# Expert rows are scaled at eviction and added into one table of token rows by an accumulating indirect DMA

## The chip, the cores and the metric

One core of one Trainium2 chip runs the whole program. The metric is the device time of one execution in microseconds; the median of three executions of the kernel before is 1866.39 us (1865.68 to 1872.32).

## What is computed

One step of a one-layer encoder for 1024 prompt tokens and 64 sample tokens (T = 1088 rows of 1024 float32). Three attention branches are mixed into a residual `h`; then comes a mixture of experts and a last normalisation. What matters here is the mixture: every token goes to 2 of 32 experts, each expert is a SwiGLU of width 512, and the two results are added to `h` with weights.

```python
def channel_mixer(h, g, w_coarse, b_coarse, w_fine, b_fine, wg, wu, wd):
    ht = rmsnorm(h, g).reshape(B * T, D)
    idx, wts = hier_route(ht, w_coarse, b_coarse, w_fine, b_fine)   # 2 experts and 2 weights for each token
    return h + moe_experts(ht, idx, wts, wg, wu, wd).reshape(B, T, D)
...
def expert_block(args):
    xblk, e = args
    return (jax.nn.silu(xblk @ wg[e]) * (xblk @ wu[e])) @ wd[e]
...
y_prompt = rmsnorm(hp, norm_final)
y_sample = rmsnorm(hs, norm_final)
```

## The kernel before, in words

The program is written in stages, each ended by a barrier of all engines. The change touches the last two.

**Mixing and routing, then the experts** (one stage, from L1736). Tokens come in nine tiles (`NT`), eight of 128 rows and one of 64. For each tile TensorE makes `h` (`project`, two halves), VectorE adds the residual into `mixT` (or `hlast` for the ninth tile), and the two engines with ScalarE normalise it (`nrow`), write it to a DRAM table `ffn_rows` and route it: `choose` finds the two experts and the logits' differences `lgd` and `dif`, `count` and `take` find the place of the token in each expert's list (`rk`, and `which`, a one-hot row over 128 places), and `enlist` multiplies `which` with `tokoh`, the token's number at its expert's column, and sums over all tiles in one PSUM bank, `TB`. At the end `toks` holds for each expert (column) the token number of each of its 128 places. A place that no token took holds 0, and so names token 0. The exponentials of `lgd` and `dif` and from them the weights `wts` are made once for all tiles, the latter in `overflow`, during the expert loop.

**Expert loop.** 32 experts, each one page of 128 places. GpSimd (POOL) gathers an expert's 128 rows from `ffn_rows` into `xe` by an indirect DMA (L1873), two buffers; TensorE turns them (`turn_x`), multiplies by gate and up weights (`up`), turns the hidden rows (`turn_h`) and multiplies by the down weights (`down`) of the expert before. Every product is made of three float32r products, so each weight is split into a high part (`hig`, ScalarE, `split_high`) and a low part (`low`, VectorE, `split_low`). SyncE's queue (SP) loads weights in halves of 1 MB into a ring of eight buffers `raw`, each load issued when TensorE has used the half eight before (`used`). ScalarE's `out` empties the banks of `down` into `ye` (two buffers), and its own queue stores the page to a DRAM table `expert_rows` (L2290). The last expert's page goes out in two halves (`last_out`). An expert with over 128 tokens would have further pages (`further`), of which there are up to 16; they are cleared with zeros by 16 DMAs early in the stage. In this case's inputs no expert has more than 128 tokens. The order within one pass is in the code of TensorE:

```python
for n in range(1, NE):
    up(n, "g", PA)
    turn_h(n - 1)
    up(n, "u", PB)
    if n + 1 < NE:
        turn_x(n + 1)
        down(n - 1)
```

**Last stage** (from L2653). POOL gathers for each token tile two tables of rows from `expert_rows`, one for each chosen expert (`ya`, `yb`, L2679, places in `sidx`); VectorE multiplies and adds them to `h` (`add`, two instructions), ScalarE makes the mean square, logarithm and exponential, VectorE scales (`scale`), SP stores.

Of the kernel before, what the change touches and what calls it, by code (L numbers as in the profile page):

```python
# [22 lines left out]
P = 128  # L23
# [4 lines left out]
NT = 9  # L28
# [48 lines left out]
def build(nc, io, stop_after=99):  # L77
# [6 lines left out]
    ysd = nc.dram_tensor("expert_rows", (SLOTS, D), F32).ap()  # L84
# [1594 lines left out]
    zfill = at("zfill", [P, SLOTS // P + 2], I32, f + 2272)  # L1679
# [11 lines left out]
    which = [at("which", [P, 2, P], F32, OS + 49152 + 1024 * i) for i in range(2)]  # L1691
    tokoh = [at("tokoh", [P, 2, NE], F32, OS + 51200 + 256 * i) for i in range(2)]
# [29 lines left out]
    toks = at("toks", [P, NE], I32, f + 32)  # L1722
    tcur = at("tcur", [P, 1], I32, f + 288)
    ye = [at("ye", [P, D], F32, o5 + 4096 * i) for i in range(2)]
# [11 lines left out]
    with Stage(nc) as ctx:  # L1736
# [5 lines left out]
            logged, picked, ranked, taken, placed, listed, filled, consts, kept0, kept1, expd, counted, found, again, halved, offset, gained, lastcopied = sems(  # L1742
                ctx, "rt", "router_in gain_in wo_high wo_low x0 x1 thigh tlow mixed hdone sq_done rooted ndone hturned ncopied "
                "logged picked ranked taken placed listed filled consts kept0 kept1 expd counted found again halved offset "
                "gained lastcopied")
        named, f0, f1, xturned, xhigh, xlow, used, high, lowed, silued, multiplied, gturned, hhigh, hlow, emptied, s0, s1, lefthalf, halfout, \
            *loaded = sems(ctx, "x", "named f0 f1 xturned xhigh xlow used high lowed silued multiplied gturned hhigh hlow "
                           "emptied s0 s1 lefthalf halfout " + " ".join(f"l{i}" for i in range(RAW)))
# [4 lines left out]
        fetched, stored = [f0, f1], [s0, s1]  # L1753
# [6 lines left out]
        def further(eng, body):  # L1760
# [3 lines left out]
            with eng.If(many > 0):  # L1764
                if eng.engine == nc.gpsimd.engine:
# [5 lines left out]
                    eng.wait_ge(again, 16 * 2 * NT)  # L1771
# [9 lines left out]
        def _(sp):  # L1781
            for i in range(STEPS):
# [26 lines left out]
            for t in range(2, NT):  # L1809
                sp.wait_ge(sq_done, t - 1)  # L1810
                sp.dma_start(xt[t % 2][0:rows_of(t), :], xp[t * P:t * P + P, :] if t < FULL else xs[:, :]).then_inc(x_in[t % 2], 16)
            sp.wait_ge(mixed, 2 * NT)
            for q in range(3, len(halves)):
                if q >= RAW:
                    sp.wait_ge(used, q - RAW + 1)
# [12 lines left out]
        def _(pool):  # L1828
# [11 lines left out]
            with pool.Fori(0, OVER) as b:  # L1840
                dst = ysd[bass.ds(b * P + NE * P, P), :].rearrange("p (a c) -> p a c", c=256)
                pool.dma_start(dst, nil[:, :].unsqueeze(1).to_broadcast([P, D // 256, 256])).then_inc(cleared, 16)
            pool.wait_ge(cleared, 16 * OVER)
# [901 lines left out]
```

## Time and profile before

| | |
|---|---|
| median of three executions | 1866.39 us |
| span of the profiled execution | 1870.5 us |
| expert loop, first to last page emptied | about 1249 to 1820 us |
| last stage | 1824 to 1870.5 us |
| TensorE busy | 1779.2 us (95%) |
| VectorE busy | 1045.1 us (56%) |
| ScalarE busy | 869.0 us (46%) |
| GpSimd busy | 115.1 us (6%) |
| bytes moved by DMA | 329.85 MB |

The profiled execution lies within the range of the three timed ones (its span of 1870.5 us is 4.1 us above their median). TensorE's busy share counts overlapping matmuls, so where it is full only means that no gap is seen. A DMA share is the time that packets took, divided by 16 engines and the stretch; it can read slightly above 1.

### The profile page before, as it was taken

To read this page: it belongs to the slowest core of one execution; us is meant where nothing else is said; L and a number is where in the kernel's file an instruction comes from. 1 tells how busy PE (TensorE), PEld (TensorE's weight loads), DVE (VectorE), ACT (ScalarE), POOL (GpSimd) and SP (SyncE) were. 2 spreads that over 40 slices of the span, in tenths; PEclk is the share of its full clock that TensorE was granted. 3 is DMA by queue.
4 is the path that set the end of the run, shared out by engine and by line. 5 is a ranking of instruction groups with operands and counts; after the bars stand their busy time and mean duration, and the time that the engine had idled before them with its cause. 6 is when DMAs were issued, how large, how long until landed. Compare 5 with 4: busy or idle time off the path is not lost. (4 is left out here: it accounts for less than half of the span.)

```text
span 1870.5 us, 25656 instructions
## 1 busy us (share of the span) xinstructions
PE 1779.2 (95%) x10354; PEld 1569.0 (84%) x10354; DVE 1045.1 (56%) x1275; ACT 869.0 (46%) x1122; POOL 115.1 (6%) x138
## 2 busy tenths in 40 slices
PE   9998999999999999999999999989999999999990
PEld 7886777888898879999999998878888888888870
DVE  5325665343245432132332245658898998988967
ACT  4224555323263331121122222247788788787853
POOL 0020000000000021000000000010000101000003
PEclk9998999999999999999999999989999999999995
DMA  5241110112112226111112142159999999999968
GB/s 186 85 110 29 29 30 12 48 34 61 34 36 81 68 59 210 40 52 45 40 48 83 46 172 71 63 212 392 414 420 410 414 410 421 418 410 416 416 232 297
DMA packets 139322, 329.85 MB, mean 176 GB/s; under 512 B 13675, under 2 KB 91335, under 8 KB 114502
## 3 DMA queue, kind: packets, MB, share of 16 engines
q1 hardware_dynamic: 123556, 272.69, 39.3%
q0 software_dynamic: 10896, 38.74, 5.6%
q10 hardware_dynamic: 4752, 16.78, 2.2%
q8 instruction: 84, 1.38, 0.3%
q14 instruction: 34, 0.27, 0.0%
HBM read 286.08 MB, written 39.87 MB: 174 GB/s over the span
## 5 line engine op out<-in xcount | busy, mean ns | idle before, releaser
L2479 DVE TENSOR_TENSOR low<-raw,hig 128x2048 fp32r<-128x2048 f32 x192 | 431.7, 2287 | 57.6 <-ACT hig L2214 57.2
L2214 ACT ACTIVATE hig<-raw 128x2048 fp32r<-128x2048 f32 x192 | 359.2, 1915 | 24.0 <-ACT ye L2287 14.4
L2042 PE MATMUL bank<-hig,xel 128*128 128x512 f32 x512 | 202.8, 396 | 0.0
L2044 PE MATMUL bank<-hig,xeh 128*128 128x512 f32 x512 | 199.9, 390 | 0.0
L2043 PE MATMUL bank<-low,xeh 128*128 128x512 f32 x512 | 199.5, 390 | 0.0
L71 PE MATMUL bank<-xhi,glo 128*128 128x384 f32 (+1 forms) x552 | 180.8, 328 | 3.2 <-ACT sg L2148 1.8
L73 PE MATMUL bank<-xhi,ghi 128*128 128x384 f32 (+1 forms) x552 | 180.8, 327 | 0.0
L72 PE MATMUL bank<-xlo,ghi 128*128 128x384 f32 (+1 forms) x552 | 180.5, 327 | 0.0
L71 PE MATMUL gproj<-xhi,glo 128*128 128x384 f32 (+1 forms) x384 | 132.6, 345 | 0.0
L72 PE MATMUL gproj<-xlo,ghi 128*128 128x384 f32 (+1 forms) x384 | 127.6, 332 | 0.0
L73 PE MATMUL gproj<-xhi,ghi 128*128 128x384 f32 (+1 forms) x384 | 127.5, 332 | 0.0
L2044 PEld LDWEIGHTS bank<-hig,xeh 128*128 128x128 f32 x512 | 96.2, 188 | 20.6
L2042 PEld LDWEIGHTS bank<-hig,xel 128*128 128x128 f32 x512 | 96.7, 189 | 19.0
L2043 PEld LDWEIGHTS bank<-low,xeh 128*128 128x128 f32 x512 | 96.4, 188 | 19.0
L2377 DVE TENSOR_TENSOR tm<-sg,bank 128x384 f32<-128x384 f32 (+1 forms) x42 | 22.3, 531 | 153.7 <-PE bank L73 153.7
L71 PEld LDWEIGHTS bank<-xhi,glo 128*128 128x128 f32 x552 | 104.2, 189 | 3.6 <-DVE glo L2351 2.0
L72 PEld LDWEIGHTS bank<-xlo,ghi 128*128 128x128 f32 x552 | 104.2, 189 | 0.0
L73 PEld LDWEIGHTS bank<-xhi,ghi 128*128 128x128 f32 x552 | 104.1, 188 | 0.0
L2068 PE MATMUL bank<-hig,htl 128*128 128x512 f32 x256 | 102.4, 400 | 0.0
L2070 PE MATMUL bank<-hig,hth 128*128 128x512 f32 x256 | 100.0, 391 | 0.0
L2069 PE MATMUL bank<-low,hth 128*128 128x512 f32 x256 | 99.9, 390 | 0.0
L2148 ACT ACTIVATE sg<-bank 128x384 f32<-128x384 f32 (+1 forms) x63 | 29.5, 471 | 142.9 <-PE bank L73 135.7
(425 smaller groups left out, 3594.5 us busy)
## 6 DMA issues: line engine op xcount, KB each, us to landing
raw<-in_w_e_gate_dram SPq DMA_DIRECT2D x64, 1024.0 KB, 7.8
raw<-in_w_e_up_dram SPq DMA_DIRECT2D x64, 1024.0 KB, 8.2
raw<-in_w_e_down_dram SPq DMA_DIRECT2D x64, 1024.0 KB, 7.4
graw<-in_w_in_dram SPq DMA_DIRECT2D x39, 512.0 KB, 3.8
expert_rows<-ye ACTq DMA_DIRECT2D x31, 512.0 KB, 8.1
xt<-in_x_prompt_dram SPq DMA_DIRECT2D x16, 512.0 KB, 3.6
expert_rows<-nil POOLq DMA_DIRECT2D x16, 512.0 KB, 10.3
braw<-in_w_branch_dram SPq DMA_DIRECT2D x24, 256.0 KB, 2.8
```

The costliest lines, as they stand in the source:

```text
L71: nc.tensor.matmul(out, wl, xh, start=(i == 0), stop=False)
L72: nc.tensor.matmul(out, wh, xl, start=False, stop=False)
L73: last = nc.tensor.matmul(out, wh, xh, start=False, stop=(i == len(parts) - 1))
L2042: nc.tensor.matmul(bank[:, :], xel[n % 2][:, kk, :], wh[:, k, :], start=(kk == 0), stop=False)
L2043: nc.tensor.matmul(bank[:, :], xeh[n % 2][:, kk, :], wl[:, k, :], start=False, stop=False)
L2044: last = nc.tensor.matmul(bank[:, :], xeh[n % 2][:, kk, :], wh[:, k, :], start=False, stop=(kk == KC - 1))
L2068: nc.tensor.matmul(bank[:, :], htl[n % 2][:, kk, :], wh[:, k, cols], start=(kk == 0), stop=False)
L2069: nc.tensor.matmul(bank[:, :], hth[n % 2][:, kk, :], wl[:, k, cols], start=False, stop=False)
L2070: last = nc.tensor.matmul(bank[:, :], hth[n % 2][:, kk, :], wh[:, k, cols], start=False, stop=(kk == 3))
L2148: nc.scalar.activation(gate_of(i, g)[:, 0:m], src[:, 0:m], ACT.Sigmoid).then_inc(gated, 1)
L2214: nc.scalar.activation(hig[q % HI][:, :], raw[q % RAW][:, :], ACT.Copy).then_inc(high, 1)
L2479: nc.vector.tensor_tensor(low[q % RAW][:, :], raw[q % RAW][:, :], hig[q % HI][:, :].bitcast(F32), ALU.subtract).then_inc(lowed, 1)
```

## The change

1. **A table of token rows.** A DRAM tensor `token_rows` (`acc`, T + 128 rows) takes the place of `expert_rows`. SP stores `h` itself there, tile by tile (`h_store`, nine DMAs, eight of 512 KB and one of 256 KB). The last 128 rows are spare. The 16 clearing DMAs become one.
2. **Weights in the same list.** For each tile ScalarE makes the exponentials (`exponents`), VectorE the weights (`weights`, five small instructions), and `enlist` sums the weights beside the token numbers; the last tile's weights follow in `enlist_weights`. The result, `slotw`, has the weight of each place; an empty place has weight 0.
3. **Empty places are marked.** Token numbers are summed as number + 1, so 0 means empty; the empty place p gets row T + p, one of the spare rows. The gather has a bound (`bounds_check=T - 1`), so places with such a row aren't fetched. `xe` is cleared once before its first use.
4. **Eviction with weight, and addition by DMA.** `out` evicts with `scale=slotw[:, n:n + 1]`, and POOL adds the page into `token_rows` by an indirect DMA with `compute_op=ALU.add` (`add_rows`), all 128 places. Each addition waits for the one before it (`added`), the first for all of `h_store`; `out` waits for the addition from its `ye` buffer.
5. **Last stage.** SP loads nine plain tiles from `token_rows`; VectorE's two instructions for `add` go.

```diff
+            def h_store(n, sem):
+                sp.dma_start(wide(acc[n * P:n * P + rows_of(n), :]), hrow(n, rows_of(n))).then_inc(sem, 16)
...
+            def add_rows(n):
+                pool.wait_ge(emptied, n + 1)
+                if n:
+                    pool.wait_ge(added, 16 * n)
+                else:
+                    pool.wait_ge(hkept, 16 * NT)
+                pool.indirect_dma_start(acc, bass.IndirectOffsetOnAxis(ap=toks[:, n:n + 1], axis=0), ye[n % 2][:, :], None,
+                                        compute_op=ALU.add).then_inc(added, 16)
             pool.wait_ge(named, 1)
             for n in range(NE):
                 if n >= 2:
                     pool.wait_ge(xturned, 2 * n - 2)
+                if n == 1:
+                    pool.wait_ge(listed, NT + 1)
+                    nc.gpsimd.memset(xe[1][:, :], 0.0).then_inc(cleanx, 1)
+                    pool.wait_ge(cleanx, 1)
                 pool.indirect_dma_start(xe[n % 2][:, :], None, htd,
-                                        bass.IndirectOffsetOnAxis(ap=toks[:, n:n + 1], axis=0)).then_inc(fetched[n % 2], 16)
+                                        bass.IndirectOffsetOnAxis(ap=toks[:, n:n + 1], axis=0),
+                                        bounds_check=T - 1, oob_is_err=False).then_inc(fetched[n % 2], 16)
+                if n >= 4:
+                    add_rows(n - 4)
+            for n in range(NE - 4, NE):
+                add_rows(n)
...
             def out(n):
                 if n >= 2:
-                    act.wait_ge(stored[n % 2], 16 * (n // 2))
+                    act.wait_ge(added, 16 * (n - 1))
+                else:
+                    act.wait_ge(scaled, 1)
                 act.wait_ge(used, place["d", n, 1] + 1)
                 for half in range(2):
-                    last = nc.scalar.activation(ye[n % 2][:, half * 512:half * 512 + 512], [Z0, Z1][half][:, :], ACT.Copy)
+                    last = nc.scalar.activation(ye[n % 2][:, half * 512:half * 512 + 512], [Z0, Z1][half][:, :], ACT.Copy,
+                                                scale=slotw[:, n:n + 1])
                 last.then_inc(emptied, 1)
-                act.wait_ge(emptied, n + 1)
-                act.dma_start(ysd[n * P:(n + 1) * P, :], ye[n % 2][:, :]).then_inc(stored[n % 2], 16)
...
+            def weights(n):
+                R = slice(0, rows_of(n))
+                ve.wait_ge(expd, n + 1)
+                nc.vector.scalar_tensor_tensor(out=wts[R, n, 0:1], in0=dif[R, n:n + 1], scalar=1.0, in1=tot[R, n:n + 1],
+                                               op0=ALU.add, op1=ALU.mult)
+                ve.drain()
+                nc.vector.reciprocal(wts[R, n, 0:1], wts[R, n, 0:1])
+                ve.drain()
+                nc.vector.tensor_tensor(wts[R, n, 1:2], wts[R, n, 0:1], dif[R, n:n + 1], ALU.mult)
+                ve.drain()
+                for k in range(2):
+                    last = nc.vector.tensor_scalar(tokoh[n % 2][R, k, NE:2 * NE], oh[R, k, n, :], wts[R, n, k:k + 1], None, ALU.mult)
+                last.then_inc(portioned, 1)
...
+            for t in range(NT):
+                r = rows_of(t)
+                sp.dma_start(ya[t][0:r, :], acc[t * P:t * P + r, :]).then_inc(ys_[t], 16)
+                if t == 0:
+                    sp.dma_start(gf[:, :], io["norm_final"].partition_broadcast(P)).then_inc(g_in, 16)
...
-            for t in range(NT):
-                r = rows_of(t)
-                for k, dst in enumerate((ya, yb)):
-                    pool.indirect_dma_start(dst[t][0:r, :], None, ysd,
-                                            bass.IndirectOffsetOnAxis(ap=sidx[k][0:r, t:t + 1], axis=0)).then_inc(ys_[t], 16)
```

POOL's program at the start of the expert loop, before: after the last tile's `ffn_rows` it holds only gathers into the two `xe` buffers, to the end of the loop.

```order
L1865 DMA ffn_rows<-nrow_7317 64x1024
L1873 DMA xe_7389<-ffn_rows,toks_7399 128x1024
L1873 DMA xe_7390<-ffn_rows,toks_7399 128x1024
L1873 DMA xe_7389<-ffn_rows,toks_7399 128x1024
L1873 DMA xe_7390<-ffn_rows,toks_7399 128x1024
```

The same place of the changed kernel (`token_rows<-ye` is an addition):

```order
L1886 DMA ffn_rows<-nrow_7317 64x1024
L1907 DMA xe_7390<-ffn_rows,toks_7400 128x1024
L1905 MEMSET xe_7391 128x1024
L1907 DMA xe_7391<-ffn_rows,toks_7400 128x1024
L1907 DMA xe_7390<-ffn_rows,toks_7400 128x1024
L1907 DMA xe_7391<-ffn_rows,toks_7400 128x1024
L1907 DMA xe_7390<-ffn_rows,toks_7400 128x1024
L1897 DMA token_rows<-ye_7406,toks_7400 1216x1024
L1907 DMA xe_7391<-ffn_rows,toks_7400 128x1024
L1897 DMA token_rows<-ye_7407,toks_7400 1216x1024
```

Each addition of page n now stands on POOL between the gathers for experts n + 4 and n + 5, and a clearing instruction stands ahead of the second gather.

VectorE at the end of routing, before: `take` of the eighth tile, the residual's last half, and, eighteen rows of the last `choose` and `take` later, the list.

```order
L2417 TENSOR_TENSOR nrow_7317<-hlast_7320,gb_7316 64x512
L2465 TENSOR_TENSOR prod_7349<-bank,oh_7331 128x64
L2467 TENSOR_TENSOR ohs_7343<-ohs_7343,oht_7344 128x32
L2469 TENSOR_REDUCE rk_7332<-prod_7349 128x2
L2472 TENSOR_SCALAR which_7364<-iot_7345,rk_7332 128x128 x2
L2397 TENSOR_TENSOR hlast_7320<-xt_7314,bank 64x512
...
L2542 CAST toks_7399<-bank 128x32
L2479 TENSOR_TENSOR low_7377<-raw_7369,hig_7385 128x2048
```

The same places of the changed kernel:

```order
L2474 TENSOR_TENSOR nrow_7317<-hlast_7320,gb_7316 64x512
L2522 SCALAR_TENSOR_TENSOR wts_7324<-dif_7335,tot_7361 128x1
L2525 RECIPROCAL wts_7324<-wts_7324 128x1
L2527 TENSOR_TENSOR wts_7324<-wts_7324,dif_7335 128x1
L2530 TENSOR_SCALAR tokoh_7367<-oh_7331,wts_7324 128x32 x2
L2536 TENSOR_TENSOR prod_7349<-bank,oh_7331 128x64
...
L2618 TENSOR_SCALAR miss_7401<-bank,empty_7404 128x32
L2620 SCALAR_TENSOR_TENSOR toks_7400<-bank,miss_7401 128x32
L2522 SCALAR_TENSOR_TENSOR wts_7324<-dif_7335,tot_7361 64x1
L2525 RECIPROCAL wts_7324<-wts_7324 64x1
```

Five small instructions of `weights` now stand ahead of `take` and of the residual's last half, the list takes two instructions instead of one, and the last tile's `weights` follow it.

## Rows read from the trace of the kernel before

**Rows 1.** The page's part 2: DMA share in 40 slices of 46.8 us.
```profile
DMA  5241110112112226111112142159999999999968
```

**Rows 2.** Stretches: engines' busy us, then PE clock, DMA share, GB/s.
```profile
1236.00:1249.00 13.00, 8.40 (x44) 7.62 (x44) 7.37 (x19) 3.56 (x4) 3.53 (x3) 0.74 1.00 410
1843.00:1855.00 12.00, 0.00 (x0) 0.00 (x0) 11.70 (x11) 4.94 (x12) 3.74 (x5) 0.50 1.03 421
...
1430.00:1500.00 70.00, 70.00 (x331) 58.61 (x331) 63.98 (x50) 56.10 (x47) 6.29 (x4) 1.00 1.01 413
```

**Rows 3.** Timeline of SP's queue: start, us; two gate loads of successive experts.
```profile
1403.39 3.05 SPq L1816 DMA_DIRECT2D raw<-in_w_e_gate_dram  x2
...
1421.15 3.05 SPq L1816 DMA_DIRECT2D raw<-in_w_e_gate_dram  x2
```

**Rows 4.** DMA queues in 1290 to 1750: packets, MB, share of 16 engines.
```profile
q1 hardware_dynamic: 22398, 163.09, 86.3%
q0 software_dynamic: 3744, 13.63, 7.4%
q10 hardware_dynamic: 3690, 13.44, 7.2%
```

**Rows 5.** Timelines of ACT, DVE and PE: the gate weights of one expert.
```profile
1412.53 3.72 ACT L2214 ACTIVATE hig<-raw 128x2048 fp32r<-128x2048 f32 x2
...
1414.70 4.48 DVE L2479 TENSOR_TENSOR low<-raw,hig 128x2048 fp32r<-128x2048 f32 x2
...
1423.67 0.39 PE L2042 MATMUL bank<-hig,xel 128*128 128x512 f32 x1
```

**Rows 6.** DMA issues of the whole run: KB each, median us to landing.
```profile
expert_rows<-ye ACTq DMA_DIRECT2D x31, 512.0 KB, 8.1
xt<-in_x_prompt_dram SPq DMA_DIRECT2D x16, 512.0 KB, 3.6
...
xe<-ffn_rows,toks POOLq DMA_INDIRECT x32, 8.7
expert_rows<-ye ACTq DMA_DIRECT2D x2, 256.0 KB, 2.0
```

**Rows 7.** Timeline of POOL and PE, then landings of `xe` in 1240 to 1260.
```profile
1243.08 1.22 POOL L1873 DMA_INDIRECT xe<-ffn_rows,toks  x1 [6.61 <-DMA ffn_rows<-nrow]
...
1257.54 1.05 PE L2028 MATMUL bank<-ident,xe 128*128 128x128 f32 x8
...
DMA to landing us min/median/max: 4.5/5.7/5.9
```

**Rows 8.** Timeline of DVE at the end of routing, and the costliest POOL memset.
```profile
1230.24 0.22 DVE L2465 TENSOR_TENSOR prod<-bank,oh 128x64 f32<-128x64 f32 x1 [0.74 <-PE bank L1964]
...
1231.64 0.68 DVE L2397 TENSOR_TENSOR hlast<-xt,bank 64x512 f32<-64x512 f32 x1 [0.20 <-PE bank L1927]
...
1241.01 0.19 DVE L2542 CAST toks<-bank 128x32 int32<-128x32 f32 x1 [1.15 <-PE bank L1974]
...
L963 POOL MEMSET keep<- 128x1088 f32 x1 | 1.0, 1010 | 76.0 <-POOLq L65 76.0
```

**Rows 9.** Timelines of the end, in order of time, and POOL's load of `ovi`.
```profile
1814.43 1.09 ACT L2287 ACTIVATE ye<-bank 128x512 f32<-128x512 f32 x2 [2.21 <-PE bank L2070]
...
1820.43 0.34 ACTq L2302 DMA_DIRECT2D expert_rows<-ye  x1
...
1824.06 0.33 SPq L2667 DMA_DIRECT2D gf<-in_norm_final_dram  x1
...
1834.66 1.06 ACT L2688 ACTIVATE junk<-ya 128x1024 f32<-128x1024 f32 x1 [9.32 <-DVE ya L2702]
...
1836.25 0.20 ACT L2692 ACTIVATE stat<-stat 128x1 f32<-128x1 f32 x1
...
1865.27 1.28 DVE L2708 SCALAR_TENSOR_TENSOR yo<-ya,stat,gf 64x1024 f32<-64x1024 f32 x1 [0.65 <-ACT stat L2692]
...
L1763 POOLq TENSOR_LOAD <-ovi x1: 509/509/509, 1791.2 to 1791.2; - x1
```

More of the change, by code:

```diff
@@ L1860, in _ @@
             pool.sem_inc(consts, 1)
-            pool.dma_start(slot_tok.rearrange("(p a) one -> p (a one)", p=P), zfill[:, :]).then_inc(filled, 16)
+            pages = slice(NE * P, SLOTS)
+            with nc.allow_non_contiguous_dma(reason="an index for each place of the overflow pages, once"):
+                pool.dma_start(slot_tok[pages, :].rearrange("(a p) one -> p (a one)", p=P), spare[:, :]).then_inc(filled, 16)
+            pool.dma_start(slot_w[pages, :].rearrange("(p a) one -> p (a one)", p=P), nought[:, :]).then_inc(filled, 16)
             for t in range(NT):
@@ L1972, in enlist, with enlist_weights @@
                 pe.wait_ge(placed, n + 1)
+                cols = slice(0, 2 * NE if n < FULL else NE)
                 for k in range(2):
-                    last = nc.tensor.matmul(TB[:, 0:NE], which[n % 2][0:rows, k, :], tokoh[n % 2][0:rows, k, :],
-                                            start=(n == 0 and k == 0), stop=(n == FULL and k == 1), skip_group_check=True)
+                    last = nc.tensor.matmul(TB[:, cols], which[n % 2][0:rows, k, :], tokoh[n % 2][0:rows, k, cols],
+                                            start=(n == 0 and k == 0), stop=False, skip_group_check=True)
+                last.then_inc(listed, 1)
+            def enlist_weights():
+                pe.wait_ge(portioned, NT)
+                pe.wait_ge(named, 1)
+                for k in range(2):
+                    last = nc.tensor.matmul(TB[:, NE:2 * NE], which[FULL % 2][0:DEC, k, :], tokoh[FULL % 2][0:DEC, k, NE:2 * NE],
+                                            start=False, stop=(k == 1), skip_group_check=True)
                 last.then_inc(listed, 1)
@@ L2017, in _ @@
             keep(16)
+            enlist_weights()
             pe.wait_ge(kept[0], 16 * 5)
@@ L2248, in _ @@
                     norm(n - 1)
+                if 2 <= n < NT:
+                    exponents(n - 2)
                 if n + 1 < NT:
@@ L2254, in _ @@
                     half_square()
+                    exponents(FULL - 1)
                 if n == NT:
@@ L2524, in _ @@
                 if n >= 2:
+                    weights(n - 2)
                     take(n - 2)
@@ L2534, in _ @@
             last_gain(0)
+            weights(FULL - 1)
             take(FULL - 1)
```

146 lines of the change are left out of this document (76 added, 70 removed).

## The prediction

> **What bounds the kernel now.** I read the page's row of DMA shares first. It is low until the 26th slice and then at nine tenths or more to the end [rows 1]: the experts keep the DMA engines full. The table by stretches says how full. In 1430 to 1500 us TensorE is busy without a gap at full clock, and the DMA share reads 1.01 at 413 GB/s [rows 2]. Where nothing but DMA limits, the share reads 1.00 to 1.03 at 410 to 421 GB/s [rows 2]: 1236 to 1249, where five weight loads, a store and two gathers wait in the queues, and 1843 to 1855, where gathers and stores of the last stage run together. So both TensorE and DMA are at their limit in the loop, and the reader should see that DMA has at most 2% to spare. The timeline of SP's queue gives the period, 1421.15 - 1403.39 = 17.76 us for each expert [rows 3], and because TensorE shows no gap this period is TensorE's. The table of queues splits the DMA load of a period: weights (q1) 86.3%, gathers (q0) 7.4%, stores of `ye` (q10) 7.2%, together 100.9% [rows 4].
>
> How late may weights be? The gate halves of one expert are split from 1412.53 on; VectorE's pair starts at 1414.70 and its first half is done about 2.24 us later, at 1416.9. TensorE takes it at 1423.67 [rows 5]. So 6.7 us of lag are covered before TensorE stops.
>
> The end is a second, separate bound: from the issue of the last store, 1820.43, to the end of the span there are 50.1 us in which TensorE has nothing to do. In them the last stage starts at 1824.06 and VectorE's last scaling is done at 1866.55 [rows 9].
>
> **The change, part by part.** The sums are against the profiled span of 1870.5 us. It is 4.1 us (0.2%) above the median of 1866.4 us, and I carry the difference over to the median.
>
> *Expert loop, DMA.* The gather loses its empty places: two experts for each of 1088 tokens make 2176 rows, 68 of 128 places for each expert, so 7.4% becomes 3.9% if all DMA engines gain alike. The store of 512 KB becomes an addition, which no row shows. At least it costs what the store does, 7.2% [rows 4]. It must also read the row in DRAM that it adds to; if reads and the write are moved in turn by the engine, a read of the same size more makes it 14.4%. I take 14.4%, since weights (a read from DRAM and a write) and stores (the same in reverse) share the engines' time as if one stream of bytes went through [rows 2, 4]. Then a period asks 86.3 + 3.9 + 14.4 = 104.6%. Against the highest reading of a full queue, 103% [rows 2], the period is 17.76 x 104.6 / 103 = 18.04 us, 0.28 longer. Page 30 is emptied at 1815.5 [rows 9], so page 0 thirty periods earlier, at 1283; from there the additions load about 29 periods, 8.1 us in all, and 6.7 of these are covered: **+1.4 us**. Bounds: at 7.2% the sum is 97.4% and nothing is lost; at 14.4% against 101% the period is 18.39 us and the loss 18.3 - 6.7 = 11.6 us.
>
> The Trainium skill (Collectives: The Full Stack, Part 3, on why ReduceScatter is half of AllGather) says that the addition itself costs a DMA engine nothing but needs two source reads on the same ring, and gives a measured ratio of 1.93. By that, an estimate from the page, the addition would be 13.9% and the loss in the loop about nothing; no row of this trace shows an addition.
>
> *Expert loop, queues.* On POOL an addition stands between two gathers. The gather for expert n + 4 is issued when TensorE has turned the rows of n + 2, just ahead of `down(n)`; page n is emptied behind `down(n)`, and POOL waits there, queued in front of the gather for n + 5. The next gather is due a period after the last, so it waits only if the addition before, which must have landed, takes over 17.8 us. Gathers of the same size land in 8.7 us and stores in 8.1 in the full loop [rows 6]; with 1.3 us more (7.2% of 17.76) for the second read I expect 10. ScalarE's `out` needs the addition of two pages before: 35 us, covered. ScalarE loses a DMA issue (0.34 us) and is not the bound: **0 us**.
>
> *Routing.* `exponents` and `weights` stand beside projections that keep TensorE full, except at the end. There five small instructions come ahead of `take`. The five like them that `take` itself has lie in the 1.4 us from 1230.24 to the residual at 1231.64 [rows 8], so I price `weights` at 1.3 us; 0.74 us of it fills an idle time and 0.2 us another [rows 8], and the residual's half, with the chain to `nrow` and the last tile's routing behind it, is some 0.4 us later. The gather for expert 0 waits for the last tile's rows in DRAM, not for the list, which is there 1.9 us earlier (1241.20 against 1243.08 [rows 7, 8]); that covers the list's second instruction, 0.3 us. `h_store` adds 256 KB to the crowded queue, 0.6 us at 410 GB/s, against some 0.5 MB less of the first two gathers. **+0.7 us.** The clearing of `xe` (1.0 us by the memset of nearly its size [rows 8]) and the wait for `enlist_weights` move the second gather from just behind the first to about 1247; with the 5.7 us of a gather here it lands by 1253 and is first needed at 1257.5 [rows 7]. The 16 clearing DMAs that go lay under full TensorE work: 0 us.
>
> *The end.* Before, 50.1 us. After: page 30 is emptied at 1815.52 [rows 9]. An addition in an empty queue is not shown; a gather of this size outside the full loop takes 4.5 to 5.9 us from POOL's issue to landing, median 5.7 [rows 7]; with 1.3 us for the second read, 7.0. Additions go one after the other: 1822.5, then 1829.5 for page 31 (emptied at 1820.4, so it no longer goes out in halves). POOL then loads `ovi` (0.5 us [rows 9]) and branches, 0.9 us, which was done at 1791 before. From the last store's landing (1820.43 + 2.0 [rows 6, 9]) to SP's first issue at 1824.06 were 1.6 us: SP starts at 1832.0, 7.9 us later than before. A plain load of 512 KB lands in 3.6 us [rows 6], 1835.6. VectorE's additions are gone, so ScalarE is the slowest: 1834.66 to 1836.45 for one tile [rows 9], with the pause 1.84, times nine 16.6 us: 1852.2. Scaling 1.3 us, and 3.95 us from there to the end as before (1866.55 to 1870.5): 1857.4. **-13.1 us.** Bounds: additions of 4.5 us each give -18; of 12 us each, -3.1.
>
> Sum: 1.4 + 0 + 0.7 - 13.1 = **-11.0 us**, a span of 1859.5 and a median of **1855.4 us**.
>
> **The rivals.**
>
> *B, the gather's saving falls on the wrong engines.* A page fills from place 0. The reference's routing of these inputs gives 50 to 92 tokens for each expert, and the first 64 places are 96% full. If a fixed half of the DMA engines serves the first 64 places, these engines keep 7.1% of gather while they carry the whole addition: 86.3 + 7.1 + 14.4 = 107.8%, and a weight load is complete when its slowest engine is. Period 18.59, 29 x 0.83 - 6.7 = +17.3 us in the loop, total +4.9: **1871 us**. The same follows if the bound doesn't spare the empty places at all. For it speaks that DMA is full; against it, that no row shows which engine serves which place. The Trainium skill (DMA: Bandwidth & Descriptors, The descriptor swizzle) has this split, engines 0 to 7 for partitions 0 to 63, for a plain transfer of 1 MiB; the trace can't show it.
>
> *C, an addition costs well over two stores: slower.* With three, 86.3 + 3.9 + 21.6 = 111.8%, period 19.28, 29 x 1.52 - 6.7 = +37.4, and 2.6 more at the end: **1894 us**. The point from which the change loses: 11.7 us saved elsewhere and 0.7 spent, so a lag of 12.4 + 6.7 = 19.1 us, 0.66 a period, 106.8%, an addition of 16.6% or 2.3 stores. If landing takes over 17.8 us POOL's chain of additions becomes the period; at 20 us that is 29 x 2.2 = +65.
>
> *D, additions are slow to land but light on the engines.* At 12 us each in the empty queue the end saves 3.1 us only, the loop is as before: -2.4, **1864 us**.
>
> **How the numbers follow.** Half a per cent, 9.3 us, is about what a measurement of this kernel can tell from no change. My forecast has 0.45, with its own range of 1849 to 1861; B 0.20; C 0.20, to 1935; D 0.15. Faster than 1857.1: two thirds of the forecast's chance, 0.30. Slower than 1875.7: a third of B, nearly all of C, 0.27. Within: 0.43. The range leaves out the best tenth of the forecast and the upper half of C: 1850 to 1893 us.
>
> **What would show it.** The interval of SP's gate loads: 17.8 to 18.1 us with no gaps in TensorE beyond a few tenths is the forecast, 18.6 is B, over 19 C. The landings of `raw` should grow by up to 6.7 us if DMA lags. The share of q0, now gathers and additions: about 18%; 11% would mean that an addition costs one store. The landing of an addition: 10 us in the loop, 7 at the end; 12 at the end is D. The last stage: SP's first load at 1832 less the routing's and loop's shift, ScalarE's chain at 1.84 us a tile, 25 us from first load to end. TensorE's granted clock should stay full in the loop; if short stalls let it fall, the loss is larger than all the sums here, and that is where I'd be wrong first.

## The result, and the profile after

| | kernel before | changed kernel |
|---|---|---|
| median, us | 1869.4 (four runs, 1865.7 to 1873.2) | 1896.0 (four runs, 1890.0 to 1898.9) |
| ratio to before, 95% interval | | 1.0141 (1.0122 to 1.0161) |
| span of the profiled execution, us | 1870.5 | 1893.8 |
| issue of the first gather, us | 1243.08 | 1238.38 |
| the last page's `ye` is emptied, us | 1820.4 | 1848.65 |
| from there to the end, us | 50.1 | 45.15 |

The change makes the kernel 1.4% slower; 0.6% faster was forecast (11.0 us of 1866.4). The profile is read as the prediction reads that of before, and splits the 23.3 us by which the span grew. The expert loop begins 3.35 us earlier (TensorE first turns gathered rows at 1245.65 instead of 1249.00), its last page is emptied 28.25 us later, so the loop itself took 31.6 us more, and the end is 4.95 us shorter: -3.35 + 31.6 - 4.95 = +23.3.

**The loop.** The table by stretches, as in [rows 2]:

```profile
1290.00:1750.00 460.00, 440.39 (x2049) 362.51 (x2048) 392.55 (x270) 350.31 (x292) 97.00 (x49) 1.00 1.01 377
1430.00:1500.00 70.00, 66.56 (x313) 54.83 (x312) 60.58 (x48) 52.49 (x45) 13.96 (x8) 1.00 1.02 368
```

TensorE had no gap in 1430 to 1500 before; now it lacks 3.4 of 70 us. The DMA share is as high as where nothing but DMA limits [rows 2], and yet only 368 GB/s move, where 413 did. The clock granted is full. SP's gate loads, as in [rows 3]:

```profile
1329.10 3.05 SPq L1833 DMA_DIRECT2D raw<-in_w_e_gate_dram  x2
...
1346.85 3.05 SPq L1833 DMA_DIRECT2D raw<-in_w_e_gate_dram  x2
...
1364.61 3.05 SPq L1833 DMA_DIRECT2D raw<-in_w_e_gate_dram  x2
...
1383.52 3.05 SPq L1833 DMA_DIRECT2D raw<-in_w_e_gate_dram  x2
...
1402.27 3.05 SPq L1833 DMA_DIRECT2D raw<-in_w_e_gate_dram  x2
```

Up to 1364.61 the period is the old 17.75 us, then 18.9, 18.75, and so on; the 22 periods from 1383.52 to 1801.61, the 10th to the 32nd and last gate load, have 19.00 us on the mean (periods of other kernels below are taken over the same 22). Additions begin at 1280.2, so five periods went by before TensorE felt anything. That fits the covered lag of the prediction, used up at 19.0 - 17.75 = 1.25 us a period (6.7 / 1.25 = 5.4). What TensorE's suppliers waited for in 1430 to 1500 (us in total, times, longest) and the queues in 1290 to 1750, as in [rows 4]:

```profile
DVE low L2550 <- ACT hig L2280: 9.5, 13, 1.9
ACT hig L2280 <- DMA raw<-in_w_e_up_dram: 8.2, 7, 1.8
ACT hig L2280 <- DMA raw<-in_w_e_gate_dram: 7.3, 4, 2.3
...
ACT hig L2280 <- DMA raw<-in_w_e_down_dram: 2.2, 4, 0.9
```

```profile
q1 hardware_dynamic: 21103, 153.66, 83.5%
q0 software_dynamic: 6923, 19.31, 17.7%
...
raw<-in_w_e_down_dram SPq DMA_DIRECT2D x49, 1024.0 KB, 14.2
raw<-in_w_e_gate_dram SPq DMA_DIRECT2D x49, 1024.0 KB, 13.1
...
xe<-ffn_rows,toks POOLq DMA_INDIRECT x25, 8.9
token_rows<-ye,toks POOLq DMA_INDIRECT x24, 11.6
```

ScalarE waits for weights (TensorE has no wait for a gather in the list of 1290 to 1815). Gathers and additions (q0) take 17.7% of the engines' time; the forecast had 18%. An addition lands in 11.6 us, far below a period, so POOL's chain of additions is not what sets the pace. The trace also has a record for each packet that a DMA engine moved. Worked out from these records over the whole run (the packets of 4096 B fall into two groups, under and over 240 ns), median durations:

```
packets of 4096 B on q0, gather or plain store:  159 ns
packets of 4096 B on q0, addition:               327 ns
packets of 8192 B on q1, weights:                309 ns
```

A row's addition takes 327 / 159 = 2.06 times what a row's store takes. A place that the gather skips is not gone from the queue: it leaves a packet of 4 B that takes 9 ns (3264 packets of 4 B on q0 in the whole run, and 1360 in e1 below, whose gather skips nothing), so skipping does spare an engine nearly the whole row.

**The head and the end.** POOL's first two gathers and the first turn of rows, as in [rows 7], then the end in order of time, as in [rows 9]:

```profile
1238.38 4.14 POOL L1907 DMA_INDIRECT xe<-ffn_rows,toks  x1 [7.51 <-DMA ffn_rows<-nrow]
1242.52 0.97 POOL L1905 MEMSET xe<- 128x1024 f32 x1
1244.29 1.03 POOL L1907 DMA_INDIRECT xe<-ffn_rows,toks  x1 [0.80 <-POOL xe L1905]
...
1245.65 1.97 PE L2086 MATMUL bank<-ident,xe 128*128 128x128 f32 x8 [4.27 <-DMA xe<-ffn_rows,toks]
...
1844.31 1.55 POOL L1897 DMA_INDIRECT token_rows<-ye,toks  x1 [15.00 <-ACT ye L2355]
...
1851.03 1.54 POOL L1897 DMA_INDIRECT token_rows<-ye,toks  x1 [5.18 <-DMA token_rows<-ye,toks]
...
1866.18 0.33 SPq L2744 DMA_DIRECT2D ya<-token_rows  x1
...
1869.73 1.06 ACT L2759 ACTIVATE junk<-ya 128x1024 f32<-128x1024 f32 x1 [2.28 <-DMA ya<-token_rows]
...
1873.26 1.06 ACT L2759 ACTIVATE junk<-ya 128x1024 f32<-128x1024 f32 x1 [1.74 <-DMA ya<-token_rows]
...
1886.86 1.28 DVE L2772 SCALAR_TENSOR_TENSOR yo<-ya,stat,gf 64x1024 f32<-64x1024 f32 x1 [0.39 <-ACT stat L2763]
```

Between the landing of the last addition (about 1857, 6 us behind its issue as those before it) and SP's first load at 1866.18 stand some 9 us. The instructions of the line that ends the expert stage show with what:

```profile
L1742 POOLq DRAIN  x1: 6174/6174/6174, 1858.6 to 1858.6; - x1
```

POOL drains for 6.17 us. Before, the same drain took 3.56 us, but at 1792.5, 28 us ahead of the last page, where nothing waited for it.

### The profile page after: what moved, and what is told of

The parts are those of the page before. It is cut to its first block and busy times, and to the rows that moved or that the text cites. A ratio compares the mean times of both kernels' runs of the same rounds, so it can differ in the third digit from the quotient of the medians.

```text
span 1893.8 us, 25725 instructions
## 1 busy us (share of the span) xinstructions
PE 1784.5 (94%) x10358; PEld 1565.5 (83%) x10358; DVE 1037.7 (55%) x1301; ACT 877.0 (46%) x1147; POOL 167.0 (9%) x141
## 5 line engine op out<-in xcount | busy, mean ns | idle before, releaser
L2550 DVE TENSOR_TENSOR low<-raw,hig 128x2048 fp32r<-128x2048 f32 x192 | 437.5, 2288 | 83.2 <-ACT hig L2280 82.5
L2280 ACT ACTIVATE hig<-raw 128x2048 fp32r<-128x2048 f32 x192 | 367.3, 1918 | 124.4 <-DMA raw<-in_w_e_gate_dram 51.7
L2101 PEld LDWEIGHTS bank<-low,xeh 128*128 128x128 f32 x512 | 96.9, 189 | 18.5
L1897 POOL DMA_INDIRECT token_rows<-ye,toks x32 | 73.5, 2298 | 273.6 <-ACT ye L2355 268.5
```

Source lines behind the costliest of these rows:

```text
L1897: pool.indirect_dma_start(acc, bass.IndirectOffsetOnAxis(ap=toks[:, n:n + 1], axis=0), ye[n % 2][:, :], None, compute_op=ALU.add).then_inc ...
L2101: nc.tensor.matmul(bank[:, :], xeh[n % 2][:, kk, :], wl[:, k, :], start=False, stop=False)
L2280: nc.scalar.activation(hig[q % HI][:, :], raw[q % RAW][:, :], ACT.Copy).then_inc(high, 1)
L2550: nc.vector.tensor_tensor(low[q % RAW][:, :], raw[q % RAW][:, :], hig[q % HI][:, :].bitcast(F32), ALU.subtract).then_inc(lowed, 1)
```

## The experiments

**The main question: do all DMA engines gain from the skipped places?** Theory 1 is rival B: a fixed half of the 16 engines serves the first 64 places, and these are full. Theory 2 is the forecast's assumption of an even load. Four kernels, made from the changed one.

e1, the gather fetches all 128 places (the tensor has 128 more rows, which are zero):

```diff
-    htd = nc.dram_tensor("ffn_rows", (T, D), F32).ap()
+    htd = nc.dram_tensor("ffn_rows", (T + P, D), F32).ap()
...
-                                        bass.IndirectOffsetOnAxis(ap=toks[:, n:n + 1], axis=0),
-                                        bounds_check=T - 1, oob_is_err=False).then_inc(fetched[n % 2], 16)
+                                        bass.IndirectOffsetOnAxis(ap=toks[:, n:n + 1], axis=0)).then_inc(fetched[n % 2], 16)
```

> The gather fetches all 128 places again (the spare rows exist and hold zeros), the rest is the changed kernel. Theory 1, rival B of the prediction: a fixed half of the 16 DMA engines serves the first 64 places of a page, these are full in both kernels, so the saving on the gather never reached the engines that bind. Then the loop's period stays at 19.05 us, and the time within 5 us of the changed kernel's 1896. Theory 2: all engines gain alike from the skipped places, and the period is long because of something else (the sum of bytes, or the addition's own cost). Then the places put back cost 3.5% of DMA time, 0.6 us a period, 19.65 us, and some 17 us in all: 1913.

e2, the addition skips the empty places too:

```diff
-                                        compute_op=ALU.add).then_inc(added, 16)
+                                        compute_op=ALU.add, bounds_check=T - 1, oob_is_err=False).then_inc(added, 16)
```

> The addition, too, leaves out the empty places (bounds on the index). Theory 1 (a fixed half of the engines serves the first 64 places, which are full): this takes work only from the half that is not the bound, the period falls by 0.1 to 0.2 us at most, to about 18.9, and the time stays above 1888. Theory 2 (even load): 47% of the addition's 60 places are gone from every engine, 6.9% of DMA time, so that the demand falls from 107% to 100%, the period to about 17.8 us, and the time by some 28 us, to 1868.

e3, the places are dealt out; `placed_at` holds for each place the rank of the token that goes there, and `which` is built from it:

```diff
+            nc.gpsimd.iota(placei[:, :], [[8, 2], [64, 2], [1, 8], [16, 4]], base=0, channel_multiplier=0)
...
+            nc.gpsimd.tensor_copy(placed_at[:, :], placei[:, :])
...
-                    last = nc.vector.tensor_scalar(which[n % 2][R, k, :], iot[R, :], rk[R, n, k:k + 1], None, ALU.is_equal)
+                    last = nc.vector.tensor_scalar(which[n % 2][R, k, :], placed_at[R, :], rk[R, n, k:k + 1], None, ALU.is_equal)
```

> The n-th token of an expert is no longer put at place n; places are dealt out so that any first part of a list lies evenly over the 16 groups of 8 places (places p with the same p // 64 and the same (p // 4) mod 8). Nothing else is changed: the addition still adds all 128 places, the gather still skips the empty ones. Theory 1: the groups are the engines', each engine then carries the mean load, 4.25 of its 8 gather packets, and the period falls from 19.05 to 18.3 us (10 engines' packets by their median durations: weights 15.3, gather 0.7, addition 2.6, last 18.7 at most), the time by 14 to 25 us, to 1871 to 1882. Theory 2 (already even): no change, 19.05 and 1896.

e4 has the edits of e2 and e3.

> Both: places dealt out evenly over the groups, and the addition leaves out the empty places. By theory 1 and by theory 2 each engine then carries 86.3% of weights, 3.9% of gather and about 7.5% of addition, 97.7%, TensorE is the bound again, the period is 17.8 us and the time about 1862. Theory 3, a per-instruction cost of the addition (POOL's issue of 2.35 us, or its chain of landings) makes the period: the period stays at 19.05 us whatever is skipped, and the time above 1890.

Measured: medians 1889.3 us (e1, ratio 1.0109, 1.0077 to 1.0140), 1890.0 (e2, 1.0103, 1.0070 to 1.0136), 1874.3 (e3, 1.0026, 1.0010 to 1.0042), 1863.5 (e4, 0.9960, 0.9944 to 0.9975). The stretch 1380 to 1780 of the changed kernel, e1, e2, e3 and e4 (400 us; TensorE's busy time is the second number):

```profile
1380.00:1780.00 400.00, 380.77 (x1764) 312.44 (x1763) 340.52 (x236) 302.85 (x252) 84.97 (x42) 1.00 1.01 374
```
```profile
1380.00:1780.00 400.00, 387.50 (x1803) 318.81 (x1801) 346.73 (x241) 309.27 (x257) 91.92 (x43) 1.00 1.02 394
```
```profile
1380.00:1780.00 400.00, 386.58 (x1797) 317.76 (x1795) 344.45 (x238) 307.91 (x256) 74.45 (x43) 1.00 1.00 367
```
```profile
1380.00:1780.00 400.00, 396.10 (x1862) 328.92 (x1861) 357.88 (x248) 317.82 (x265) 83.37 (x44) 1.00 1.02 394
```
```profile
1380.00:1780.00 400.00, 400.00 (x1892) 335.25 (x1891) 362.20 (x251) 322.01 (x270) 60.38 (x45) 1.00 1.01 388
```

Theory 1 holds. e3 moves the same bytes with the same instructions in the loop as the changed kernel and differs, but for building the table once, only in which place a token has: its period is 18.05 us against 19.00, its time 22 us less. The even load of the forecast gave 18.04; e3 has the load that the forecast had computed. (Its profiled execution took 3.7 us less than its median, so the agreement to 0.01 us is in part luck.) e2 takes 47% of the addition's rows away and stays above 1888, since they come off engines that were not full. e1, against theory 2's 1913, puts 60 places back and is not slower (but nearly 7 us below the changed kernel's median, outside the 5 us of its expectation). With places spread, skipping them in the addition gives what it should: TensorE is full again in e4. Theory 3 of e4 falls with it, POOL issues as many additions in the same order.

The loop, from TensorE's first turn of gathered rows to the last page's eviction, took 571.4 us before, 603.0 in the changed kernel, 578.7 in e3 and 571.1 in e4. So dealing out the places takes 24.3 of the 31.6 us away, and e3 still loses 7.3 us where the forecast had 1.4.

Theory 1 does not say why e1 is faster than the changed kernel. e5 repeats the changed kernel unedited, in another sitting:

> The changed kernel once more, in the same hour as the others, because the kernel that fetches all places came out 6.7 us faster than it, which no theory has. If that was the day or the chip, this run gives about 1890 and a period near 18.65 us, which is what engines 0 to 7 would need with full halves (weights 15.3 + gather 1.2 + addition 2.6 = 19.1, over the 1.03 that the share shows when queues are full). If skipping places does cost something by itself (an empty place, a longer issue on POOL), it gives 1896 and 19.0 again.

It gave 1895.0 us (1.0128, 1.0094 to 1.0161) and 19.0 us again, so the difference is the kernel's. It is taken up below.

**Which places belong to one engine?** e6 is e4 with another dealing, even over eight places in a row:

```diff
-            nc.gpsimd.iota(placei[:, :], [[8, 2], [64, 2], [1, 8], [16, 4]], base=0, channel_multiplier=0)
+            nc.gpsimd.iota(placei[:, :], [[1, 16], [16, 8]], base=0, channel_multiplier=0)
```

> As e4 (dealt out, additions skip empty places), but the n-th token stands at place 8 x (n mod 16) + n / 16: evenly over the 16 groups of eight places in a row. If an engine serves eight places in a row, this is as even as e4, 1863 and a period of 17.75 us. If engine e serves places 4j to 4j+3 and 32 places on from them in one half (the grouping that e3 and e4 assumed, from the Trainium skill's DMA: Bandwidth & Descriptors, The descriptor swizzle), the first 64 tokens fill eight of the engines wholly and the others not at all, as in e2: a period of about 18.7 us and 1885 to 1890.

Measured: 1885.5 us (1.0081, 1.0052 to 1.0110), period 18.55 us, against 1863.5 and 17.75 of e4. Eight places in a row are not an engine's; places 4j to 4j + 3 with those 32 further on fit both. The Trainium skill (DMA: Bandwidth & Descriptors, The descriptor swizzle) states that grouping for a plain transfer of 1 MiB; the runs agree with it for indirect gathers and indirect additions of 4 KB rows (17.75 us with e4's dealing, 18.55 with e6's). No packet record names its engine, so the grouping is inferred from the periods.

e12 deals in turn to the two halves (its additions skip the empty places, and it has the early drain of e9, which comes below):

```diff
+            nc.gpsimd.iota(placei[:, :], [[1, 2], [2, 64]], base=0, channel_multiplier=0)
```

> e9 with a simpler dealing: even ranks to places 0, 1, 2 ... of the lower half, odd ranks to those of the upper half. If it is only the halves that count (within one, the first 32 places give each of its eight engines four), this is as good as e9: a period of 17.75 us, no gaps in TensorE, 1859. If the load has to be even over eight places in a row, each half has four groups full and four nearly empty, and the period is that of e6, 18.65 us, 1882.

Measured: 1868.0 us (0.9995, 0.9983 to 1.0008), period 18.06 us on the mean, in between. My "only the halves count" was too simple: 34 tokens in a half give its first engine four places and then two more, places 32 and 33. For a list of 68 that engine carries 6 gathers and 6 additions, where e4's carry 4.25 on the mean, and a list of 92 (46 in a half) fills it to 8. The fullest engine decides, not the fuller half. The packets of e4's additions give the length of every list (50 to 92). With 14.8 us of weights for each engine (48 packets of 309 ns), 159 and 327 ns for each gathered and each added row of the fullest engine, and never less than TensorE's 17.75, the estimate for e12 is 18.06 us on the mean of the lists, what was measured; the same sum gives e3 18.2, 0.15 too much, so part of that agreement is luck.

**The second read.** e8 stores instead of adding, so it leaves out the sum over experts and the residual:

```diff
-                pool.indirect_dma_start(acc, bass.IndirectOffsetOnAxis(ap=toks[:, n:n + 1], axis=0), ye[n % 2][:, :], None,
-                                        compute_op=ALU.add).then_inc(added, 16)
+                pool.indirect_dma_start(acc, bass.IndirectOffsetOnAxis(ap=toks[:, n:n + 1], axis=0), ye[n % 2][:, :], None).then_inc(added, 16)
```

> The addition becomes a plain indirect store onto the token's row, so this kernel leaves out the summation over experts and the residual. Everything else is the changed kernel. By the forecast's step (the second read makes the addition cost two stores) its packets take 159 ns in place of 327, q0's share falls from 17.7 to about 11%, and even the fuller engines carry 15.3 + 1.2 + 1.3 = 17.8 us: the period is TensorE's, 17.75 us, and the time about 1860. If the order on POOL and not the engines' load makes the loop long, the period stays near 19 us. An idle-queue landing of about 5 us against 6.1 for the addition.

Measured: 1860.8 us (0.9944, 0.9922 to 0.9966), every period 17.75 us, packets of 159 ns, and:

```profile
q0 software_dynamic: 7484, 20.84, 11.4%
...
token_rows<-ye,toks POOLq DMA_INDIRECT x26, 8.8
```

As expected: without the second read even the fuller engines have room.

**The clears.** e7 puts the 16 clearing DMAs back, into a tensor that nobody reads:

```diff
+    pagesd = nc.dram_tensor("pages", (OVER * P, D), F32).ap()
...
-            pool.wait_ge(cleared, 16)
+            with pool.Fori(0, OVER) as b:
+                dst = pagesd[bass.ds(b * P, P), :].rearrange("p (a c) -> p a c", c=256)
+                pool.dma_start(dst, nil[:, :].unsqueeze(1).to_broadcast([P, D // 256, 256])).then_inc(cleared, 16)
+            pool.wait_ge(cleared, 16 * OVER + 16)
...
```

> The changed kernel with the 16 clearing DMAs of 512 KB put back (into a tensor that nobody reads). The prediction gave them nothing. The profiles of before and after differ by about 3 us ahead of the first gather: if the clearing DMAs are the cause, the first gather is issued 3 us later than in the changed kernel, the mixing stage's matmul gap of 1.8 us near 729 us is back, and the time is 3 us longer. If not, the same.

Measured: 1906.4 us (1.0182, 1.0147 to 1.0216). The first gather is issued at 1242.38 instead of e5's 1238.71, 3.7 us later. The waits of e7 in 715 to 745:

```profile
ACT ghi L2192 <- DMA graw<-in_w_in_dram: 13.8, 2, 10.5
...
ACT bhi L2197 <- DMA braw<-in_w_branch_dram: 11.8, 1, 11.8
...
PEld bank L71 <- DVE glo L2412: 2.9, 1, 2.9
```

In the changed kernel ScalarE waits 6.6 us for `graw` and 4.7 for `braw`, and TensorE not at all; in the kernel before they are 9.4, 12.0 and 2.0 us. So the clears held up both loads of weights of the mixing stage, and TensorE waited behind `graw`, by way of its split into `ghi` and `glo`. Lying under full TensorE work did not make them free, since the work's own weights queue behind them. The time grew by 11.4 us, not by 3. Against e5's trace 3.9 us came before TensorE's first turn of gathered rows, 7.2 in the loop (2.9 of them in the 22 periods, 19.14 us against 19.01) and 0.3 after it. Only the first part is the one expected; why the loop changes, with one tensor more in DRAM, is not explained, and where the tensors lie in DRAM was not varied by itself.

**The drain.** e9 is e4 with `pool.drain()` right behind the issue of the last addition:

```diff
             for n in range(NE - 4, NE):
                 add_rows(n)
+            pool.drain()
             pool.wait_ge(xturned, 2 * NE)
             pool.wait_ge(added, 16 * NE)
```

> e4 with one more instruction: POOL drains right after it has issued the last addition, while that is in flight, before it waits for its landing. In the changed kernel and in e4 a drain of 6.17 us stands on POOL between the landing of the last addition and the barrier that lets SP start the last stage; the forecast of the end had no such term. If the drain's time is work that goes on beside the transfer (the descriptors' rings being emptied), the drain at the stage's end falls below 1 us and SP's first load comes 5 to 6 us earlier: 1858. If the time is a wait that begins only when a drain is met behind a landed transfer, both drains take 6 us or the first stretches past the landing: 1863 to 1866.

> e4 again beside e9, on the same chip: 1862 to 1865, 0.3 to 0.5% below the kernel before. It is there so that the difference to e9 is taken from one sitting.

Measured in one sitting: e9 1858.9 us (0.9951, 0.9933 to 0.9969), e10, which is e4 again, 1860.2 (0.9960, 0.9944 to 0.9976). The two times are not told apart, since their intervals overlap. The traces are: from the last addition's issue to SP's first load e4 and e10 take 14.57 and 14.43 us, e9 and e12, which has its drain, 11.57 and 12.23. For e4 and then for e9 follow the timeline's rows of POOL's last addition and SP's first load, and the drains from the instructions of a line (1744 ends the stage, 1918 is the new drain):

```profile
1818.10 1.54 POOL L1901 DMA_INDIRECT token_rows<-ye,toks  x1 [3.89 <-DMA token_rows<-ye,toks]
...
1832.67 0.33 SPq L2748 DMA_DIRECT2D ya<-token_rows  x1
```
```profile
L1744 POOLq DRAIN  x1: 6175/6175/6175, 1825.1 to 1825.1; - x1
```
```profile
1818.45 1.54 POOL L1901 DMA_INDIRECT token_rows<-ye,toks  x1 [4.03 <-DMA token_rows<-ye,toks]
...
1830.02 0.33 SPq L2749 DMA_DIRECT2D ya<-token_rows  x1
```
```profile
L1918 POOLq DRAIN  x1: 8846/8846/8846, 1818.2 to 1818.2; - x1
```
```profile
L1744 POOLq DRAIN  x1: 127/127/127, 1828.5 to 1828.5; - x1
```

The stage's end comes 11.57 us behind the issue instead of 14.57: 3.0 us gained, half of what I expected. The early drain takes longer, 8.85 us, of which the first 1.8 are the issue itself (its row starts at 1818.2, the issue's at 1818.45 and lasts 1.54): it ends at 1827.1, 8.6 us behind the issue, where e4's ends at 1831.3, 13.2 us behind it. It is neither free beside the transfer nor a wait that begins only at the landing.

**The 0.4 us a period that the sum doesn't have.** The fullest engine's load for each period is the weights, 15.3 us (86.3% of 17.76 [rows 4]), plus its rows: full places 7.7 of 8 on the mean, 4.25 when spread. Over 1.03, the highest reading of a full queue [rows 2], as in the prediction:

| kernel | fuller engines | emptier engines | fuller / 1.03 | measured period | TensorE idle in 1380 to 1780 |
|---|---|---|---|---|---|
| e3 | 18.6 | 18.6 | 18.08 | 18.05 | 3.9 |
| e1 | 19.2 | 19.2 | 18.65 | 18.67 | 12.5 |
| e6 | 19.1 | 15.7 | 18.5 | 18.55 | 11.4 |
| e2 | 19.1 | 15.7 | 18.5 | 18.76 | 13.4 |
| changed, e5 | 19.2 | 18.1 | 18.6 | 19.00, 19.01 | 19.2 |

These are estimates. Packets' medians alone, without the 1.03, give nearly the same: 14.8 us of weights and so 18.7 for the fuller engines and 18.1 for e3. The sum fits the even kernels to 0.03 us, e6 and e2 to 0.05 and 0.26, and falls 0.4 short in the changed kernel. Three more runs ask with what that goes. e11 is the changed kernel and begins each list at place 64 (`[[-64, 2], [1, 64]], base=64` in the iota of e3); e13 is e3 with the dealing of e6; e14 is e1 with the bounds of e2.

> The changed kernel (additions add all places) with each list begun at place 64 instead of 0: the n-th token stands at place (n + 64) mod 128. Now the groups of the upper half are full and those of the lower half nearly empty. If the two halves of the engines are alike in all else, nothing changes: a period of 19.0 us and 1895, as e5. It bears on the 0.3 us a period by which the changed kernel (18.95) is longer than e1, e2 and e6 (18.65 to 18.72), whose fuller engines carry the same: if the lower half's engines also carry something else (the instructions' loads, say), the period falls to about 18.65 here and the time to 1889.

> The changed kernel (gather skips, addition adds all places) with the places of e6: the first 64 tokens fill eight engines of the sixteen, four in each half. The fuller engines carry 19.2 us a period as in e5, so 18.6 by the sum. e5, e7 and e11 need 19.0 to 19.1, e1, e2 and e6 18.55 to 18.76. If what makes the difference is a gather that is short on half the engines beside an addition that is full on all, this gives 19.0 to 19.1 and 1893 to 1899; if it is that whole halves (places 0 to 63 against 64 to 127) differ, it gives 18.6 and 1886.

> The mirror: the gather fetches all places, the addition skips the empty ones, each list begins at place 0. The fuller engines again carry 19.1 to 19.2 us, the emptier ones 15.3 + 1.3 + 0.1 = 16.7. If any unevenness between the engines costs 0.3 us above the sum, the period is 19.0 and the time 1895; if only the short gather beside the full addition does, it is 18.6 to 18.7 and 1888 to 1890.

Measured: e11 1898.7 us (1.0171, 1.0146 to 1.0195), period 19.14; e13 1895.0 (1.0139, 1.0117 to 1.0160), 18.99; e14 1893.4 (1.0121, 1.0089 to 1.0154), 18.72. Their rows for 1380 to 1780, in that order:

```profile
1380.00:1780.00 400.00, 377.08 (x1758) 309.81 (x1757) 337.29 (x232) 301.31 (x251) 84.43 (x42) 1.00 1.01 371
```
```profile
1380.00:1780.00 400.00, 381.54 (x1774) 314.02 (x1773) 341.31 (x236) 303.10 (x253) 81.49 (x43) 1.00 1.01 375
```
```profile
1380.00:1780.00 400.00, 385.32 (x1797) 316.22 (x1795) 345.86 (x240) 308.31 (x256) 77.06 (x43) 1.00 1.01 381
```

So it is neither the lower half's engines (e11) nor the halves as such (e13), nor any unevenness (e14, by the period; its time lies between the two expectations). It comes with a gather that is short on half of the engines beside an addition that is full on all: four kernels of that kind lie at 19.0 to 19.14 us, four others with the same fuller engines at 18.55 to 18.76. Each period is that of one profiled execution, and the second group alone spreads over 0.2 us; the gap between the groups is 0.2. By what mechanism stays open.

## Why the prediction was wrong, step by step

- **What bounds the kernel: right. The covered lag of 6.7 us: right for the changed kernel only.** There stalls began after five periods of additions, and five is what 6.7 us cover; the landings of `raw` grew from 7.9, 8.3 and 7.7 us (gate, up, down) to 13.1, 14.1 and 14.2. But e3, at 0.30 us a period, should by the same term lose 29 x 0.30 - 6.7 = 2.0 us and lost 7.3. Why the cover was so thin there was not tried.
- **The addition costs two stores: right.** 327 ns against 159, 2.06; q0's share 17.7% against 18%. e8 shows it by taking the second read away. The estimate from the Trainium skill (Collectives: The Full Stack, Part 3), 1.93, is near it too. Rival C came out at 1894, close to the time measured, but by a cost of three stores that no packet shows: a right number for a wrong reason.
- **"7.4% becomes 3.9% if all DMA engines gain alike": the step that failed.** The prediction names the other case as rival B and gives it 0.20. The engines of the first 64 places kept their gathers: e1, which puts the skipped places back, has no longer a period (18.67 against 19.00), and e3, which spreads the gain, has the forecast's (18.05 against 18.04) and is 22 us below the changed kernel in time. In the loop that is 24.3 of the 31.6 us. I had a fact that speaks for B (first 64 places 96% full) and, in the Trainium skill (DMA: Bandwidth & Descriptors, The descriptor swizzle), the grouping for a plain transfer, and weighed both below a mean over 16 engines, for want of a row. A mean share can't speak for or against it. With this step right the forecast would still have been missed: e3's ratio is 1.0026, +5 us where -11 was forecast. Its trace, 1.6 us under that of before, has +7.3 in the loop (forecast +1.4), -4.5 at the end (-13.1) and the first turn of rows 4.3 us early (+0.7).
- **B's size: too small as well.** 18.59 us and +17.3 in the loop against 19.00 and +31.6. By the measured period, 29 x 1.25 - 6.7 = 29.6 of the 31.6. 0.4 us a period, 29 x 0.4 = 12 us, is the part of this that stays open, and so do the 2 us left. B's mechanism alone, with its own sum of 1871, would also have missed the 1896.
- **Queues, 0 us: right.** Additions land in 11.6 us (forecast 10), under a period, and TensorE never waits for a gather.
- **The clears, 0 us: wrong, in the kernel's favour.** The first gather is issued 4.7 us earlier than before, where the forecast had 0.7 later, and by e7 3.7 of these are the clears'. Of the 4.7, TensorE got 3.35: the first gather's issue takes 4.14 us on POOL against 1.22 [rows 7]. e1, whose gather skips nothing, has 4.70 there, so the bounds aren't the cause; what is was not tried.
- **The end, -13.1: the additions right, two terms missing.** They landed in some 6 us each (forecast 7). SP started 17.5 us behind the last page instead of 11.6: the drain's 6.17 us, which I had not seen; before, it took 3.56 us and lay under the experts. From SP's start to the end 27.6 us passed, not 25.4: the second tile's load came 1.74 us late and the last stores took 5.66 us against 3.95, while a tile cost ScalarE 1.67 us instead of 1.84. In sum -4.95.
- **The clock, named as the first thing that could go wrong: it did not.** In the changed kernel the granted clock was 1.00 from 1260 to 1849 us but for 3.4 us at the lower level, from 1730.5 on (below).

## What to carry to other kernels

When DMA is within a few per cent of its limit, add up the load of the fullest of the 16 engines, place by place, and not the mean: a page filled from place 0 puts its rows on half of the engines, and what is skipped then saves nothing. Dealing the places evenly, which costs a table on the chip, turned this change from 1.4% slower to 0.4 or 0.5% faster than the kernel before (e4, e9 and e10, the best found). And when a change moves POOL's last work to the end of a stage, its drain comes along; drained right behind the last issue, the stage ended some 3 us earlier here by the traces, which the times are too coarse to show.

## What was unexpected of the hardware

- A drain on POOL behind an indirect addition takes 6.17 us even when the addition has landed, and the same in e4 (6.175); behind the plain indirect store of e8 it takes 6.26. Issued right behind the addition it takes 8.85, and the one after it 0.13.
- Long packets are frequent where engines have room to spare and rare where all are full. Counted from the packet records in 1430 to 1700, weight packets of 8192 B that took over 400 ns, where 309 is the median:

```
changed kernel                               432 of 10933
e2 (half the engines emptier)                582 of 11091
e4 (all engines with room, TensorE limits)   528 of 11702
kernel before (the same, with less room)     256 of 11690
e1 (all engines equally full)                 13 of 11129
e3 (all engines equally full)                 16 of 11479
```

  So the DMA share reads 1.00 to 1.01 in the changed kernel, e2 and e4 too, and can't tell a full engine from one with room. That an engine which waits for its next piece shows as a long packet would explain it, but isn't shown. Between kernels that move the same bytes GB/s tells them apart: 374 against e3's 394.
- TensorE's pauses in the loop brought short falls of its clock, but not each time. By the matmul records of 1290 to 1810, pauses of 2.02 us (changed kernel), 2.20 (e1), 2.24 (e2), 2.76 (e13) and 2.81 (e5) were followed, within 1.3 us, by 3.4 us at the lower of the two levels, 1.2 GHz; pauses of 2.12 (e7) and 2.46 (e11) were not. In e5 the loop went better behind it:

```profile
1558.00:1560.00 2.00, 0.00 (x0) 0.00 (x0) 2.00 (x3) 1.46 (x1) 0.00 (x0) 1.00 1.03 428
1560.00:1565.00 5.00, 4.68 (x14) 3.73 (x15) 5.00 (x4) 4.47 (x4) 1.13 (x1) 0.66 0.80 337
1565.00:1570.00 5.00, 5.00 (x25) 4.20 (x24) 4.61 (x3) 4.47 (x5) 1.67 (x1) 1.00 0.91 288
```

  The mean of 0.66 over 5 us is 3.4 us at half the clock. That period took 22.45 us, the next three 17.75 or 17.76 and the fifth 19.02: 94.7 us for five, not more than five at 19.0 (95.0). The DMA share falls to 0.80 and 0.91 behind the pause, which fits weights that have caught up.
